# 51 groups of matrix products behind the last layer of a two-block transformer kernel

## What is computed

```python
def sq_relu_mlp(h, w_in, w_out):
    return jnp.square(jax.nn.relu(h @ w_in)) @ w_out
...
        x = x + gt1 * rms_norm(y_lat, g_mix_post[i])
        m_lat = sq_relu_mlp(modulate(rms_norm(x, g_mlp_pre[i]), sh2, sc2), w_mlp_in[i], w_mlp_out[i])
        x = x + gt2 * rms_norm(m_lat, g_mlp_post[i])
```

## Time and profile before

| | us |
|---|---|
| runs | 3466.33 and 3465.70, median 3466.01 |
| span of the profiled execution | 3464.7 |
| PE busy in it | 3413.6 |

### The profile page before, as it was taken

The page is one execution under the profiler, slowest core; times in us unless marked ns, Lnnn a source line. Parts: engine busy times, 40 slices in busy tenths (PEclk is TensorE's granted clock), DMA queues, the critical chain, the costliest instruction groups (busy, mean ns, idle before and its releaser), DMA issues.

```text
span 3464.7 us, 46915 instructions
## 1 busy us (share of the span) xinstructions
PE 3413.6 (99%) x18494; PEld 2874.5 (83%) x18494; DVE 2165.7 (63%) x3570; ACT 1318.4 (38%) x1951; POOL 298.0 (9%) x376
## 2 busy tenths in 40 slices
PE   9999999999999999999999999999999999999998
PEld 7888967898888988896789888899988898588888
DVE  7555565656555655666577777888776556655444
ACT  4222463333222422245333523355533236643222
POOL 0000232001000100023100000012100001210000
PEclk9999999999999999999999999999999999999999
DMA  7444302434444344320243444344444311013221
GB/s 279 188 158 163 107 24 101 163 129 168 158 162 151 134 169 158 148 106 12 101 164 140 149 150 170 146 147 182 172 174 165 117 66 68 25 50 112 96 98 48
DMA packets 85561, 452.01 MB, mean 130 GB/s; under 512 B 10304, under 2 KB 12544, under 8 KB 48608
## 3 DMA queue, kind: packets, MB, share of 16 engines
q1 hardware_dynamic: 83168, 439.10, 34.2%
q0 software_dynamic: 2176, 9.92, 0.8%
HBM read 446.88 MB, written 2.10 MB: 130 GB/s over the span
## 4 chain that ended last, share of the span: by engine, by line
PE 84%; DVE 7%; ACT 3%; issue 2%; DMA 2%; POOL 0%; SPq 0%; DVEq 0%; ACTq 0%; POOLq 0%
PE ps L662 21%; PE ps L663 21%; PE ps L664 21%; DVE WL L568 2%; DMA araw<-in_ast 2%; PE ps L2778 1%; PE ps L2780 1%; PE ps L2779 1%; PE ps L3477 1%; PE ps L1039 1%; PE ps L1040 1%; PE ps L1041 1%; ACT P L1859 1%; PE ps L1776 1%; PE ps L1299 1%
## 5 line engine op out<-in xcount | busy, mean ns | idle before, releaser
L662 PE MATMUL ps<-nH,WH 128*128 128x512 f32 x2256 | 880.3, 390 | 0.4 <-ACT rot L3207 0.4
L664 PE MATMUL ps<-nH,WL 128*128 128x512 f32 x2256 | 877.8, 389 | 0.0
L663 PE MATMUL ps<-nL,WH 128*128 128x512 f32 x2256 | 877.8, 389 | 0.0
L568 DVE TENSOR_TENSOR WL<-raw,WH 128x2048 fp32r<-128x2048 f32 (+2 forms) x297 | 651.6, 2199 | 361.5 <-ACT WH L557 360.0
L557 ACT ACTIVATE WH<-raw 128x2048 fp32r<-128x2048 f32 (+2 forms) x299 | 543.2, 1822 | 561.1 <-PE ps L664 479.9
L662 PEld LDWEIGHTS ps<-nH,WH 128*128 128x128 f32 x2256 | 423.5, 188 | 90.6 <-issue 3.3
L664 PEld LDWEIGHTS ps<-nH,WL 128*128 128x128 f32 x2256 | 423.4, 188 | 88.3
L663 PEld LDWEIGHTS ps<-nL,WH 128*128 128x128 f32 x2256 | 423.5, 188 | 87.2 <-issue 0.2
L628 DVE SCALAR_TENSOR_TENSOR araw<-araw,cB 128x1024 f32<-128x1024 f32 x224 | 275.6, 1230 | 205.6 <-DMA araw<-in_ast 205.2
L662 PE MATMUL ps<-hH,WH 128*128 128x512 f32 x944 | 368.8, 391 | 2.5 <-DVE ma L2454 1.4
L664 PE MATMUL ps<-hH,WL 128*128 128x512 f32 x944 | 367.4, 389 | 0.0
(11 more groups left out here) (452 smaller groups left out, 5940.0 us busy)
## 6 DMA issues: line engine op xcount, KB each, us to landing
raw<-in_wst SPq DMA_DIRECT2D x273, 1024.0 KB, 4.8
araw<-in_ast SPq DMA_DIRECT2D x225, 512.0 KB, 5.7
raw<-in_wst SPq DMA_DIRECT2D x18, 512.0 KB, 3.3
araw<-in_wst SPq DMA_DIRECT2D x9, 1024.0 KB, 4.8
row<-in_ast SPq DMA_DIRECT2D x15, 512.0 KB, 10.5
cw<-in_cw POOLq DMA_DIRECT2D x4, 1024.0 KB, 5.9
h<-in_xT SPq DMA_DIRECT2D x4, 512.0 KB, 5.6
raw<-in_wst SPq DMA_DIRECT2D x8, 256.0 KB, 2.6
```

Of the source, the lines that this page charges most:

```text
L568: dve.q.tensor_tensor(M.WL[k % NW][:, 0:n], M.raw[raw_use[k]][:, 0:n], M.WH[k % NW][:, 0:n].bitcast(F32), ALU.subtract).then_inc(*v_wlo.up(k))
L662: pe.q.matmul(to, hi[:, i, cc], xh, start=i == 0, stop=False)
L663: pe.q.matmul(to, hi[:, i, cc], xl, start=False, stop=False)
L664: t = pe.q.matmul(to, lo[:, i, cc], xh, start=False, stop=i == nk - 1)
```

## The change

PE's program gets one more function, `behind_pe`, after `rest_pe`. It first waits for all of `v_h`, so for the fourth add of half B. Then it issues 51 groups. A group is four times three products (one group: twice three) that accumulate in one bank of six in turn, and then one float32 product of the tile of ones, 128x128, into bank 7. No engine reads these banks, no semaphore is raised, and nothing else in the kernel differs. The groups differ in how the operands are addressed:

| groups | columns | moving operand | weights | bank written |
|---|---|---|---|---|
| 4 | 512 | forward, backward, backward, forward | plain | forward, backward, forward, backward |
| 9 | 512 | backward, 4 to 56 columns on | plain | backward |
| 9 | 512 | forward, 2 to 56 columns on | plain | forward |
| 3 | 512 | plain (one: the high part alone) | one column repeated; one tile throughout; plain | forward |
| 1 | 512 | columns 0, 256, 1, 257, ... (`two`) | plain | forward |
| 1 | 512 | the first two columns, 256 times (`same`) | plain | forward |
| 1 | 256 | the tile of ones as bfloat16 | the same | forward |
| 1 | 512 | plain, as float32, six products | plain, as float32 | forward |
| 1 | 512 | another tensor, `hH2` and `hL2` | plain | forward |
| 8 | 256 | forward, 0 to 56 columns on | plain | forward |
| 8 | 256 | backward, 0 to 56 columns on | plain | backward |
| 1 | 384 | plain | plain | forward |
| 4 | 512 | plain | every 2nd, 3rd, 4th, 8th column | forward |

```diff
+        def behind_pe(pe):
+
+            for i in range(8):
+                pe.wait_ge(*v_h.to("latmlp1postA", i))
+                pe.wait_ge(*v_h.to("latmlp1postB", i | 1))
+            hi, lo = [M.WH[0][:, 128 * i:128 * i + 128] for i in range(4)], [M.WL[0][:, 128 * i:128 * i + 128] for i in range(4)]
+            count = [0]
+
+            def group(moves, weigh, out, n=4):
+
+                b = banks[count[0] % 6]
+                count[0] += 1
+                for i in range(n):
+                    (xh, xl), (wh, wl) = moves(i), weigh(i)
+                    pe.q.matmul(out(b), wh, xh, start=i == 0, stop=False, skip_group_check=True)
+                    pe.q.matmul(out(b), wh, xl, start=False, stop=False, skip_group_check=True)
+                    pe.q.matmul(out(b), wl, xh, start=False, stop=i == n - 1, skip_group_check=True)
+                pe.q.matmul(banks[7][:, 0:128], M.ones[:, :], M.ones[:, :], start=True, stop=True)
+
+            def rows(h, l, shift=0, N=S, back=False):
+                flat = [t[:, :, :].rearrange("p a b -> p (a b)") for t in (h, l)]
+                cut = lambda i: slice(S * i + shift, S * i + shift + N)
+                if back:
+                    return lambda i: tuple(t[:, cut(i)][:, ::-1] for t in flat)
+                return lambda i: tuple(t[:, cut(i)] for t in flat)
+
+            plain = lambda i: (hi[i], lo[i])
+            ahead, back = (lambda b: b[:, 0:S]), (lambda b: b[:, 0:S][:, ::-1])
+            n = lat.nH, lat.nL
+            group(rows(*n), plain, ahead)
+            group(rows(*n, back=True), plain, back)
+            group(rows(*n, back=True), plain, ahead)
+            group(rows(*n), plain, back)
+            for shift in (4, 8, 16, 20, 24, 32, 40, 48, 56):
+                group(rows(*n, shift=shift, back=True), plain, back)
+            for shift in (2, 4, 8, 16, 24, 32, 40, 48, 56):
+                group(rows(*n, shift=shift), plain, ahead)
+            one = lambda t: t[:, 0:1].broadcast_to([128, 128])
+            group(rows(*n), lambda i: (one(hi[i]), one(lo[i])), ahead)
+            group(rows(*n), lambda i: (hi[0], hi[0]), ahead)
+            group(lambda i: (lat.nH[:, i, :], lat.nH[:, i, :]), plain, ahead)
+            two = lambda t: t.rearrange("p (a b) -> p b a", a=2)
+            group(lambda i: (two(lat.nH[:, i, :]), two(lat.nL[:, i, :])), plain, ahead)
+            same = lambda t, i: t[:, i, 0:2].unsqueeze(1).broadcast_to([128, 256, 2])
+            group(lambda i: (same(lat.nH, i), same(lat.nL, i)), plain, ahead)
+            halves = M.ones[:, :].bitcast(BF16)
+            group(lambda i: (halves[:, 0:256],) * 2, lambda i: (halves[:, 0:128],) * 2, lambda b: b[:, 0:256])
+            group(lambda i: (lat.nH[:, i, :].bitcast(F32), lat.nL[:, i, :].bitcast(F32)),
+                  lambda i: (hi[i].bitcast(F32), lo[i].bitcast(F32)), ahead, 2)
+            group(rows(M.hH2[:, 0], M.hL2[:, 0]), plain, ahead)
+            half, back_half = (lambda b: b[:, 0:S // 2]), (lambda b: b[:, 0:S // 2][:, ::-1])
+            for shift in (0, 8, 16, 24, 32, 40, 48, 56):
+                group(rows(*n, shift=shift, N=S // 2), plain, half)
+                group(rows(*n, shift=shift, N=S // 2, back=True), plain, back_half)
+            three = lambda b: b[:, 0:384]
+            group(rows(*n, N=384), plain, three)
+            for step in (2, 3, 4, 8):
+                apart = lambda i, m=step: (M.WH[0][:, 512 * i:512 * i + 128 * m:m] if 512 * i + 128 * m <= 2048 else
+                                           M.WH[0][:, 0:128 * m:m],) * 2
+                group(rows(*n), apart, ahead)
+
@@ -3705,6 +3766,7 @@
             rest_pe(pe, attention2_pe(pe))
+            behind_pe(pe)
```

## The result

| | before | after |
|---|---|---|
| runs, us | 3466.33, 3465.70 | 3595.13, 3597.87 |
| median, us | 3466.01 | 3596.50 |
| span of the profiled execution, us | 3464.7 | 3593.3 (its run: 3595.13) |

The ratio is 1.0374, 95% interval [1.0352, 1.0396]: slower by 130.5 us. Predicted were 3598.3 us, within 3591 to 3642.

A forecast was written before the change was run, and what follows sets the result against it. PE, busy 3413.6 of 3464.7 us, was taken as the bound: start 3462.15 + products 130.2 + clock 1.9 + `two` 2.4 + end 0.4 = 3597.0 us span; with 1.3 to the median, 3598.3, range 3591 to 3642.

The forecast's parts named there:

- The main step: Behind the fourth add PE runs alone, so the kernel's end is its stream's end, priced by the products' paces.
- The start: Fourth add ends at 3462.09 us; PE starts the new stream 0.06 us later, at 3462.15.
- Stream and end: After the stream: 0.16 us for the last record and about 0.2 us to the span's end, together 0.4.
- The clock: Stream starts at 1.2 GHz, rising 2.9 to 4.8 us later; loss 1.5 to 2.4 us, taken as 1.9.
- Backward and shifted: Groups read or written backward, and shifted ones, keep the ordinary pace: nothing extra; ordinary backward pace given 0.62.
- sign of being wrong: Prediction fails if a forward, contiguous group is not at 2.94 us once the clock is up, or any group stalls.
- The rival of two beats: Backward products take two beats a column, 5.4 us a group: 35.8 us more, 3634, or 3636.5 either direction; chance 0.22.
- `two`: the step that failed: Group reading columns 0, 256, 1, 257: priced as a float32 record, 2.4 us extra, between 0 and 7.6.
- Stepped weights: Four groups with weights at steps: load hidden beside 512-column products, nothing extra; 5.1 us if wholly open.
- Not run: Rival: build or load drops the unread products, PE ends at L882, time 3466 us; chance 0.02.
- low clock throughout: Rival: stream granted 1.2 GHz throughout, about 130 us more, 3727; chance 0.05 together with four beats.

The follow-up runs named there:

- third experiment: Changed kernel with its groups replaced by 35 whose moving operand mostly alternates between two places, plus two DVE and two ACT bank reads: 3568.48 us.
- fifth experiment: Changed kernel with its 51 groups replaced by 29, ordinary beside turned operand (columns 0, 256, 1, 257), varying weight and moving columns: 3536.64 us.
- second experiment: Changed kernel plus twelve products of ones in front of PE's wait for the last add: 3595.76 us.

## Why the prediction was right

The main step held: PE is alone behind the fourth add and never idle (127.00 of 127 us in the window above), so the time is the sum of the paces. By parts, in us from the first product of one group to that of the next, of the profiled execution:

| part | by the prediction | measured |
|---|---|---|
| first group, with the low clock | 2.94 + 1.9 = 4.84 | 5.18 |
| 11 groups of 512 reading backward | 32.4 | 33.28 |
| 9 shifted, reading forward | 26.5 | 27.11 |
| 5 others of 512, read forward, weights not stepped | 14.7 | 14.87 |
| `two` | 2.94 + 2.4 = 5.34 | 2.81 |
| `same` | 2.94 | 2.90 |
| bfloat16; float32 | 1.66; 5.37 | 1.53; 5.29 |
| 16 groups of 256; 384 columns | 26.6; 2.30 | 26.31; 2.31 |
| 4 with stepped weights | 11.8 | 12.65 |
| whole stream | 134.5 | 134.2 |

The parts agree better in the sum than one by one: `two` was taken 2.5 us too dear, and backward reading, shifts, stepped weights and the clock together 2.7 too cheap. That these cancel to 0.3 us is luck.

- *The start.* Forecast 3462.15, found 3458.68. The wait behind the add was 0.14 us and not 0.06; the rest is the front of the kernel, which ran 3.5 us quicker in this execution. The runs give no sign that the change did that: with other products in the same place the fourth add ended at 3458.9 (third experiment) to 3463.6 (fifth). The profiled run stood 1.8 us above its own span, where the prediction had 1.3. Stream and end alone give 134.9 by the prediction and 134.6 measured.
- *The clock.* The rise came 4.8 us after the first product, as in the earlier trace rows, and cost 2.2 to 2.3 us, inside 1.5 to 2.4. The second experiment showed that it is the clock and not the wait.
- *Backward and shifted.* 3.02 to 3.03 against 2.97 for plain forward groups: 0.06 us a group when it is read backward, nothing when it is written backward (2.96). But the shifted groups that are read forward took 2.98 to 3.03 too, so the 0.06 is not shown to belong to the direction, and each of these nine groups took 0.07 us more than the 2.94 forecast. Of its sign of being wrong, a forward group away from 2.94, this much came true. The rival of two beats, 5.4 us a group, falls.
- *`two`: the step that failed.* The prediction took 2.4 us, between 0 and 7.6, and reasoned that a column not beside its neighbour takes longer and that nothing can be quicker than one column a beat. The group was 0.16 us quicker than an ordinary one. The ordinary product was not at one column a beat: 512 columns in 0.2267 us are 0.94 of a column per cycle of 2.4 GHz, while 216 ns are 0.99. The slack in what looked like a limit was 5%. What the ordinary product waits for stays open (fifth experiment).
- *Stepped weights.* At steps of 2, 3, 4 and 8 the groups took 3.02, 3.10, 3.17 and 3.28 us from one product of ones to the next. The records of their loads last 0.25, 0.31 and 0.33 us at steps 3, 4 and 8, and 0.19 at step 2 as in plain groups. So from step 3 on part of the longer load lies open; the four groups cost 0.8 us more than the prediction's nothing, which had 5.1 as its other end.
- *Not run, low clock throughout.* All 714 records are there, and the clock was 1.00 from 3464 on.

## What to carry to other kernels

Work behind the last real instruction is priced by the paces of one engine; take them from rows with the same columns and type and add the climb of the clock. Here the sum of 134.5 us came within 0.3, but single terms were off by up to 2.5. When one engine is busy 99%, measure its pace against the best form of the same instruction before taking it as a floor: reading the moving operand in two alternating halves, with the bank emptied in the same order, made this kernel 2.7% faster at no cost to DVE and ACT. A form has to be tried by itself: pairs instead of single columns made a product four tenths slower.

## What the hardware showed that was not expected

- An fp32r product of 512 columns runs at 216 ns when its moving operand alternates between two places 4 to 1024 columns apart, or stays within 4 columns; in order it takes 227 to 234, in pairs 328, at every 2nd column 453. At 512 columns the weights' number of columns has no part in it.
- The emptying of a bank at every second column is free: 682 ns became 681 on DVE, 597 became 592 on ACT.
- Under weights of 128 columns, products of 64 and of 128 columns had one pace, 112 ns, whatever the order of the operand, and turned ones of 256 columns had it too, so turning pays only above that.
- Twelve products of ones ahead of a wait of 1.8 us kept the clock at 2.4 GHz through it.
